# Prompt attention of a two-layer decoder step, regrouped by whole head and branch

## What is computed

```python
def masked_softmax(s, mask):
    s = jnp.where(mask, s.astype(F32), NEG)
    m = jnp.max(s, axis=-1, keepdims=True)
    p = jnp.where(mask, jnp.exp(s - m), 0.0)
    return p / jnp.maximum(jnp.sum(p, axis=-1, keepdims=True), 1e-30)
...
    # 16 heads of 64 in 4 groups; kc, vc: means of 32 keys, 16 blocks for the prompt
    p_c = masked_softmax(s_c, c_end[None, :] <= qpos[:, None])
    o_c = jnp.einsum('bkgtc,bckd->btkgd', p_c, vc)
...
    p_s = masked_softmax(s_s, m_s)        # selected keys
    p_w = masked_softmax(s_w, (dpos >= 0) & (dpos < WINDOW) & (win_pos[None, :] >= 0))
    return (gates[..., 0:1] * o_c + gates[..., 1:2] * o_s + gates[..., 2:3] * o_w)
```

## Time and profile before

| what | us |
|---|---|
| median of three runs (2410.69 to 2412.24) | 2410.81 |
| profiled execution | 2415.41 |
| its span | 2413.6 |
| NSA projection, from its first to the next stage's first instruction | 1080 to 1252 |
| prompt attention | 1290 to 1648 |

### The profile page before, as it was taken

The page is one execution under the profiler, slowest core; times in us unless marked ns, Lnnn a source line. Parts: engine busy times, 40 slices in busy tenths (PEclk is TensorE's granted clock), DMA queues, the critical chain, the costliest instruction groups (busy, mean ns, idle before and its releaser), DMA issues. The chain is left out here.

```text
span 2413.6 us, 38555 instructions
## 1 busy us (share of the span) xinstructions
PE 1904.6 (79%) x11902; PEld 1362.6 (56%) x11902; DVE 961.1 (40%) x2346; ACT 521.3 (22%) x1285; POOL 218.7 (9%) x368
## 2 busy tenths in 40 slices
PE   5999877887884878749976788785699889577775
PEld 4888766776673544438854565552244447544443
DVE  1776434435113111131336667674466530311112
ACT  2113823323101111110023333332101100111110
POOL 0000012222102111100000000000000000121110
PEclk8999968888885999969997878887699999689997
DMA  3666451100152999834742101002698841669995
GB/s 113 215 217 206 155 175 38 37 1 36 63 198 101 390 424 423 352 118 152 214 139 94 41 26 53 26 26 92 193 306 272 260 151 53 253 238 425 425 420 217
DMA packets 168255, 442.80 MB, mean 183 GB/s; under 512 B 25905, under 2 KB 97074, under 8 KB 151026
## 3 DMA queue, kind: packets, MB, share of 16 engines
q1 hardware_dynamic: 113954, 384.02, 43.5%
q10 hardware_dynamic: 43216, 39.99, 5.3%
q0 software_dynamic: 11008, 17.89, 2.0%
HBM read 426.09 MB, written 44.03 MB: 195 GB/s over the span
## 5 line engine op out<-in xcount | busy, mean ns | idle before, releaser
L1653 PE MATMUL moe_experts_bank_gu<-moe_weights_gu,moe_experts_xT 128*64 128x256 f32 x2048 | 260.1, 418 | 68.5 <-DMA moe_weights_gu<-in_w_gate_up 45.2
L1653 PEld LDWEIGHTS moe_experts_bank_gu<-moe_weights_gu,moe_experts_xT 128*64 128x64 f32 x2048 | 173.5, 151 | 167.0 <-issue 116.5
L392 PE MATMUL proj_acc<-h_gdn,proj_w 128*128 128x272 f32 x1024 | 238.8, 396 | 13.9 <-DMA proj_w<-in_gdn_w 13.9
L392 PEld LDWEIGHTS proj_acc<-h_gdn,proj_w 128*128 128x128 f32 x1024 | 196.3, 192 | 55.2 <-DMA proj_w<-in_gdn_w 14.4
L1891 PE MATMUL nproj_acc<-nsa_h,nproj_w 128*128 128x272 f32 x640 | 147.6, 394 | 0.0
L1734 DVE SCALAR_TENSOR_TENSOR moe_experts_h<-moe_experts_bank_gu,moe_table,moe_experts_gate 128x128 f32<-128x128 f32 x64 | 22.4, 351 | 304.1 <-ACT moe_experts_gate L1698 304.1
L1674 PE MATMUL moe_experts_bank_y<-moe_weights_down,moe_experts_hT 128*64 128x512 f32 x512 | 116.9, 598 | 25.8 <-ACT moe_experts_hT L1703 25.8
L1891 PEld LDWEIGHTS nproj_acc<-nsa_h,nproj_w 128*128 128x128 f32 x640 | 122.0, 191 | 25.3
L2543 PE MATMUL satt_out_acc<-satt_values,satt_pT 128*64 128x256 f32 x512 | 120.0, 392 | 0.0
L2131 PE MATMUL patt_scores<-nsa_proj,patt_q 128*128 128x128 f32 (+3 forms) x256 | 106.7, 552 | 0.0
L265 DVE TENSOR_REDUCE first_sums<-proj_raw 128x2048 f32 (+1 forms) x32 | 73.1, 2286 | 79.7 <-DMA proj_raw<-in_cmp_pool 79.7
(11 more groups left out here) (425 smaller groups left out, 3150.5 us busy)
## 6 DMA issues: line engine op xcount, KB each, us to landing
moe_weights_gu<-in_w_gate_up SPq DMA_DIRECT2D x64, 2048.0 KB, 21.1
moe_weights_down<-in_w_down SPq DMA_DIRECT2D x64, 1024.0 KB, 22.4
proj_raw<-in_cmp_pool SPq DMA_DIRECT2D x128, 256.0 KB, 3.5
satt_keys<-in_slc_pool SPq DMA_DIRECT2D x256, 128.0 KB, 3.1
satt_values<-in_slc_pool ACTq DMA_DIRECT2D x256, 128.0 KB, 3.3
nproj_raw<-in_cmp_pool SPq DMA_DIRECT2D x80, 256.0 KB, 3.5
proj_w<-in_gdn_w SPq DMA_DIRECT2D x32, 512.0 KB, 3.6
patt_raw<-in_cmp_pool SPq DMA_DIRECT2D x48, 256.0 KB, 2.9
```

The lines of the kernel that those rows point to most:

```text
L392: mm = pe.matmul(acc[s][:, a, 0:HALF], w[s][:, k, :], g.hT[:, k, a * HALF:(a + 1) * HALF], start=(k == 0), stop=(k == KT - 1))
L1653: mm = pe.matmul(gu_bank[m][H, 0:FF], ln.xT[:, k, H], w.gu[:, k, m * FF:(m + 1) * FF], start=(k == 0), stop=(k == KT - 1))
```

## The change

Prompt attention is rewritten, without loops. A **unit** is one pair of heads (i = 0 to 7) and one branch (selected or window): 16 units, each over all 512 queries.

- Scores: `q` and POOL's scaling are gone. The two heads' scores are matmuls of 64 rows, one on partitions 0 to 63 and one on 64 to 127, into different banks.
- `causal_neg` is widened to 512 columns, and one DVE operation adds it, scales by -1/8, writes the result to SBUF and keeps the row's minimum (mask, scale and negated maximum in one pass). A second instruction reads out the kept value. ACT's exponential undoes the sign.
- The sums of a unit (8 columns) are floored, inverted and gated once per unit. POOL multiplies the identity by them into `diag`, 8 diagonal tiles, and the turn is a matmul of the probabilities by that tile, so that scaling and transposing are one step. The turn is a fp32 matmul, no longer a transpose.
- Turned tiles are gathered by key tile b: for b the query tiles b to 3 go to one bank, ACT copies lane 0 and DVE lane 1, and one matmul per lane multiplies by the values, 64 columns wide, lane 0 into partitions 0 to 63 of the bank `out`, lane 1 into 64 to 127.
- The compressed branch is done once for all heads near the stage's start; its result is added by one matmul per head.
- Scores run two units ahead (AHEAD = 2).
- Page sums: 3, 8 and 0 pages a step instead of 4, 4 and 3.
- The constants grow by 515 columns (264 KB).

The diff, cut to its core (what is removed from the stage is the code printed above):

```diff
-PAGES_GDN = 4
-PAGES_NSA = 4
-PAGES_ATT = 3
+PAGES_GDN = 3
+PAGES_NSA = 8
...
+ATT_UNITS = 2 * Q_TILES
+AHEAD = 2
+SCORE_BUFFERS = AHEAD + 1
+TURNED = 3
...
+                def score(u, t):
+                    i, _ = of_unit(u)
+                    n = (t + 1) * P
+                    for ln in lanes:
+                        if u or t >= 2:
+                            before = f"{u} {t - 2}" if t >= 2 else f"{u - 1} {t + 2}"
+                            pe.wait_ge(ln.masked.sem, ln.masked.past(before))
...
+                    for ln in lanes:
+                        pe.matmul(ln.scores[t % 2][:, 0:n], g.proj[ln.R, i, t * P:n], g.proj[ln.R, key_tile(u), 0:n],
+                                  start=True, stop=True).then_inc(*ln.scored.done(f"{u} {t}"))
+                def turn(u, b):
+                    if b == 0:
+                        pe.wait_ge(spread.sem, spread.past(f"{u}"))
+                    for ln in lanes:
+                        bank = turned_bank(u, b, ln.s)
+                        use = 2 * (TILES * u + b) + ln.s - TURNED
+                        if use >= 0:
+                            other = lanes[use % 2].copied
+                            pe.wait_ge(other.sem, other.past(f"{use // (2 * TILES)} {use // 2 % TILES}"))
+                        for t in range(b, TILES):
+                            mm = pe.matmul(bank[:, (t - b) * P:(t - b + 1) * P],
+                                           tile_of(ln.p[u % SCORE_BUFFERS], t)[:, b * P:(b + 1) * P],
+                                           diag[u % 2][:, ln.s, t, :], start=True, stop=True)
+                        mm.then_inc(*ln.turn.done(f"{u} {b}"))
+                def multiply(u, b):
+                    i, a = of_unit(u)
+                    pair = i // GROUP
+                    for ln in lanes:
+                        pe.wait_ge(ln.copied.sem, ln.copied.past(f"{u} {b}"))
...
+                        mm = pe.matmul(out[ln.R, b * P:SEQ], g.v_rows[:, a, b, at:at + HD],
+                                       ln.pT[u % 2][:, KEYS_AT[b]:KEYS_AT[b + 1]], start=(a == 0 and b == 0),
+                                       stop=False)
...
+                for t in tiles:
+                    score(0, t)
+                for pair in range(2):
+                    for j in range(GROUP):
+                        for t in tiles:
+                            for ln in lanes:
+                                at = ((pair * TILES + t) * GROUP + j) * P_BLOCKS
+                                mm = pe.matmul(turned[ln.s][:, at:at + P_BLOCKS],
+                                               g.proj[ln.R, pair * GROUP + j, t * P:(t + 1) * P], g.kc[ln.R, pair, :],
+                                               start=True, stop=True)
...
+                for u in units:
+                    if u == 1:
+                        turn_cmp()
+                    for b in tiles:
+                        if u + AHEAD < ATT_UNITS:
+                            score(u + AHEAD, b)
+                        turn(u, b)
+                        if b:
+                            multiply(u, b - 1)
+                        elif u:
+                            multiply(u - 1, TILES - 1)
+                multiply(ATT_UNITS - 1, TILES - 1)
...
+                        dve.tensor_tensor_reduce(
+                            out=tile_of(ln.p[u % SCORE_BUFFERS], t), in0=ln.scores[t % 2][:, 0:n],
+                            in1=g.const("causal_neg")[:, SEQ - n:SEQ], scale=-(HD ** -0.5), scalar=BIG, op0=ALU.add,
+                            op1=ALU.min, accum_out=neg_max[u % SCORE_BUFFERS][:, ln.s, t:t + 1]
+                        ).then_inc(*ln.masked.done(f"{u} {t}"))
...
+                for u in units:
+                    if u + 1 < ATT_UNITS:
+                        weigh(u + 1)
+                    for b in tiles:
+                        if u + AHEAD < ATT_UNITS:
+                            mask(u + AHEAD, b)
+                        copy(u, b)
+                        if u == 0 and b == 1:
+                            weigh_cmp()
...
+                    pool.tensor_tensor(diag[u % 2][:, :, :, :].rearrange("p s t q -> p (s t) q"),
+                                       ident.unsqueeze(1).broadcast_to([P, 2 * TILES, P]),
+                                       x.unsqueeze(2).broadcast_to([P, 2 * TILES, P]), ALU.mult
+                                       ).then_inc(*spread.done(f"{u}"))
...
+                    for b in tiles:
+                        copy(u, b)
+                        if u + AHEAD < ATT_UNITS:
+                            soften(u + AHEAD, b)
+                        if b == 0 and u and u % 2 == 0:
+                            place(u // 2 - 1)
```

More of the change, by code:

```diff
@@ L58 @@
 NEG = -1e30
+BIG = 3e38
 SEL_BIG = 1e6
@@ L125, in constants @@
     c["token"] = np.arange(TILES + 1)[None, :] * P + r[:, None]
-    c["causal_neg"] = np.where(r[None, :] <= r[:, None], 0.0, NEG)
+    c["causal_neg"] = np.where(np.arange(SEQ)[None, :] - (SEQ - P) <= r[:, None], 0.0, NEG)
     blocks = SEQ // CMP
@@ L2060, in prompt_attention_stage @@
         lanes = []
+        names = [f"{u} {t}" for u in units for t in tiles]
         for s in range(2):
@@ L2083, in prompt_attention_stage @@
[L2083 to L2098 removed]
+            ln.p = [st.sb(f"p{s}{n}", [P, TILE_AT[TILES]]) for n in range(SCORE_BUFFERS)]
@@ new lines, in prompt_attention_stage @@
+        multiplied = st.line("multiplied", names)
+        weighed = st.line("weighed", [f"{x} {u}" for u in units for x in ("floor", "inverse", "gate")])
+        spread = st.line("spread", [f"{u}" for u in units])
+        finished = st.line("finished", [f"{i}" for i in range(Q_TILES)])
+        placed = st.line("placed", [f"{i}" for i in range(Q_TILES)])
+        cmp_pe = st.line("cmp_pe", ["scores", "values", "turned 0", "turned 1"])
+        cmp_dve = st.line("cmp_dve", ["masked", "max", "values", "sum", "floor", "inverse", "gate"])
```

389 lines of the change are left out of this document (202 added, 187 removed).

## The result

The changed kernel takes 2286.1 us (median of four runs, 2282.7 to 2290.0) where the kernel before took 2411.5 in the same comparison (four runs): a ratio of 0.948, 95% interval 0.9464 to 0.9497, 125 us less. The forecast was 2284 us, 127 less. The total is right to 2 us, the parts are not: two terms were too dear or too cheap by more than 10 us, in opposite directions. The profiled execution of the changed kernel is one of 2282.7 us, with a span of 2280.9.

The account below looks back on a forecast made before the run. PE was expected to bound the rewritten prompt attention, which no engine filled before. Terms -144 (attention), +17 (page sums in the NSA projection) and +0.6 (constants) gave -127 us, from 2410.8 to 2284 us; range 2250 to 2330.

Parts of the forecast that it names:

- start, first score to first turn: Start of prompt attention, covered by nothing: 41 us before the first turn, 24 of them compressed matmuls; bounds 24 to 45.
- first turn to the end of the stage: Rest of prompt attention: 14 units of 10.85 us, two without scores of 8.1, and small remainders.
- prompt attention in all: Whole prompt attention stage: 214 us against 358, 144 us less.
- NSA projection and its end: Four more page sums a step: 7.8 us a step, +8.6 over 18 steps, +8 at the end; +17 together.
- constants, DeltaNet projection: 264 KB more constants cost +0.6 us in the first stage; a page less in a DeltaNet step gives nothing.
- PE becomes the bound, nearly without gaps, at full clock: Prompt attention: PE's 10.85 us a unit exceeds every other engine's work, at a clock of 1.00.
- Rivals 2 and 4: Prompt attention: 2, PE waits for the others, 2308 us, chance 0.12; 4, TensorE stays at 1.2 GHz, 2424, chance 0.04.
- Both pairs overlap: Prompt attention's two-head matmuls on PE run side by side: scores and values each 2.15 us a unit, 4.31 in line.
- Rival 1: Prompt attention: pairs of scores run in line, +34 us, 2318 us; chance 0.13.
- A unit of 10.85 us: PE's time per prompt attention unit: scores, turns, values, compressed branch and changes of shape; 15.6 us if all in line.
- change of shape: PE switching between scores, turns and values: 12 changes a unit at 0.14 us, 1.68 us.
- DVE 7.1, ACT at most 9.7, POOL 1.91: Other engines' us per prompt attention unit, all under PE's 10.85; keeping the minimum taken as 0.8 of DVE's.

Follow-up runs that it names:

- line_scores: Changed kernel, but both heads of a pair take scores from the first head's queries and keys, so on the same array rows: 2327.9 us, ratio 0.9654.
- turn_once: Changed kernel, but the turn is a one-pass transpose that leaves out the weighing by gate and sum: 2249.6 us, ratio 0.9315.
- first_turn: Changed kernel, but the first unit's weights and diagonals are made ahead of the compressed branch's work: 2284.1 us, ratio 0.945.
- half_sums: Changed kernel, but each page sum in the NSA projection takes only half of its 16 positions, all pages still loaded: 2273.9 us, ratio 0.9433.
- old_moved: Kernel before, with its old prompt attention, but page sums moved to 3, 8 and none: 2440.7 us against 2408.1, ratio 1.0115.
- best: Changed kernel with weighing on POOL, one-pass turns, first unit's weights first, and page sums back at 4, 4 and 3: 2223.2 us, ratio 0.9214.
- best_fewer: The same as best, plus scores of two query tiles taken together, 10 changes of shape a unit and not 12: 2217.2 us, ratio 0.9188.
- sums_back: Changed kernel, but page sums at 4 and 5 in turn (DeltaNet), 4 (NSA), 2 a unit of prompt attention: 2264.5 us, ratio 0.9398.
- pool_scale: Changed kernel, but POOL multiplies the softened tiles by gate over sum and the turn is a one-pass transpose, no diagonals: 2248.9 us, ratio 0.932.

## Why the prediction came out right

| term | forecast, us | measured, us | |
|---|---|---|---|
| start, first score to first turn | 41 | 27.7 | too dear by 13 |
| first turn to the end of the stage | 173 | 178.4 | too cheap by 5 |
| prompt attention in all | 214 (-144) | 208 (-151) | |
| NSA projection and its end | +17 | +28.5 | too cheap by 11 |
| constants, DeltaNet projection | +0.6 | 0 to -2 | |
| sum | -127 | -123 to -125 | medians: -125 |

The sum of the measured terms is -151 + 28.5 and 0 to -2, -123 to -125. The two profiled executions differ by 133 us (spans 2413.6 and 2280.9), since before's is 4 us above its median and after's 3 below; the experts' two stages, which the change doesn't touch, hold some 8 of them (251 and 248 us before, 246 and 245 after).

Step by step:

1. *PE becomes the bound, nearly without gaps, at full clock.* Right. It is busy from first turn to end, at a granted clock of 1.00 from 1344 us on; behind the first turn line_scores and turn_once moved the stage by PE's own time (2.14 us a unit more, 2.46 less). Rivals 2 and 4 fall with it: no copy or mask holds PE, and the clock did not stay at half.
2. *Both pairs overlap.* Right, and line_scores shows it for the scores by taking it away. Rival 1's +34 us is what that run adds behind the first turn (32). The quadrants of the earlier trace rows were the right row to lean on.
3. *A unit of 10.85 us.* It is 10.96 and 11.82 in turn, 11.4 in the mean. The columns were right to a hundredth of a microsecond. The term that was mis-sized is the change of shape: 0.14 us from the earlier trace rows, measured 0.20 into scores, 0.20 into turns, 0.15 into values, 2.2 us a unit for 1.7. The earlier trace rows showed only the changes among value matmuls, the cheapest of the three.
4. *DVE 7.1, ACT at most 9.7, POOL 1.91.* They are 6.0, 6.5 and 1.9. The unknown, the read-out of the minimum, is far below the ACT row that I bounded it by (0.197 us); of the two groups

```profile
L2224 DVE CUSTOM_DVE_ANT_0 patt_p<-patt_scores,consts 128x512 f32<-128x512 f32 x32 | 20.8, 688 | 19.9 <-PE patt_scores L2132 19.8
...
L2224 DVE DVE_READ_ACCUMULATOR2_ANT patt_neg_max<- 128x1 f32 x128 | 10.5, 82 | 0.0
```

the second is its price, 82 ns; the mask itself takes the 0.68 us of a plain one.
5. *The start, 41 us.* Here the step failed that chose 24 us for the compressed matmuls, near the in-line end, "since PE is lightly loaded there". They take 11.1, with the clock at full for 3 of them. In first_turn, at a clock of 0.50 throughout, they take 13.7, 0.107 each, half of the 0.218 of the earlier trace rows at that clock: by this rate the pairs overlap at half clock too, though no run took the overlap away here as line_scores did for the scores. I had taken overlap for the scores and not for these, on no row. The other end that the text gave, 7.1, was too cheap: it took 0.111 us for a pair, a price of passes of 128 columns at full clock.
6. *The NSA projection, +17.* The mechanism was named (a buffer is loaded and summed within two steps) but not summed: 6.9 us of SP, 4.6 of DVE and the landing, which I left as what remains. The loop was 16.4 us, 8.2 a step and not 7.8, of which landing takes the other 5: +15.7 us in the projection for 8.6. The end is two such trips with nothing beside them, +12.8 for +8. half_sums shows the loop, old_moved that the new attention has no part in it.
7. *DeltaNet projection, nothing for a page less.* 0 to 2 us less: the gates stage starts at 300.1 us for 302.5. Executions with three pages a step put it at 299.3 to 303.0, those with four (before, best, best_fewer) at 302.5 to 303.5, so the page is worth little more than the spread. At four and five in turn (sums_back, 307.0) the cover has ended.

So the number was right because 13 us too dear at the start of the attention went against 5 in its units and 11 in the projection. Each lay inside the bounds that the text gave; that they cancelled to 2 us is luck.

What the change itself gave: some 151 us from the new attention, less 28 for the page sums. The fold of the weights into the turn cost some 35 us of what could have been had (turn_once 34, pool_scale 36 from the first turn on, less 3.6 at its start).

## What to carry to other kernels

When a stage becomes bound by one engine, price every pass on that engine: a fold that saves another engine's work (here two passes for one, 2.46 us a unit) is a loss if an idle engine, here POOL, can do that work beside it. Work that is moved under "cover" has to be summed as a round trip (issue, landing, use, release of the buffer), not as a share of each queue; it was that loop that bound, while each engine in it had time left. And price a change of the array's shape by the pair of shapes: the cheapest one seen is not the price of all.

## What the runs showed of the hardware

- Two fp32 matmuls on different 64-row halves of the array, both 128 columns wide, run side by side in full: 1.06 us for four passes of 512 columns with the change of shape, 1.91 when both use the same rows.
- A DVE mask with a running minimum costs the plain mask's time and 82 ns for the read-out, where ACT's read-out of a sum takes 188 to 197.
- At the start of prompt attention the granted clock is at half (1.2 GHz) in every run, with a spell at full of about 3 us in some and not in others, and it goes to full for good 26 to 46 us in; the same first scores and compressed passes took 15.1 us in one execution and 18.3 in another. What decides on the spells the runs don't tell. Differences of 3 us at the start of a stage therefore say little about an edit.
- DVE's masks of 512 columns on PSUM took 689 ns with POOL busy for 60% on products of 128x512 tiles, and 688 with POOL at 20%: no measurable loss on DVE's side.
- A fp32 tile of 128x128 turned by a matmul with a diagonal takes two passes of 0.111 us, by a transpose one of 0.108 (turn_once: groups of 8, 6, 4 and 2 in 1.02, 0.80, 0.59 and 0.37 us from start to start).
